# A chunked recurrence written out over one short and four long chunks, in place of a loop over six chunks of 88

## The chip, the cores and the metric

The kernel runs on one core of a Trainium2 chip. The metric is the device time of one execution in microseconds (us); each kernel is timed in several runs and the median is quoted. TensorE (PE in the rows) multiplies, VectorE (DVE) and ScalarE (ACT) work elementwise and copy results out of the accumulator memory (`ps`), GpSimd (POOL) and the DMA queues take no part in the stage that changes.

## What is computed

The reference is a two-block hybrid network on 512 tokens with 16 meta tokens in front (528 positions). The change is in one branch of the second block, a gated delta rule with 4 heads of width 128, run once forward and once backward over the positions. In the reference's words, for each chunk of positions:

```python
decay_mask = jnp.exp(jnp.where(lower, diff, -jnp.inf))
m = jnp.where(strict, jnp.einsum('bhnck,bhnsk->bhncs', k_beta, k) * decay_mask, 0.0)
t = lax.linalg.triangular_solve(eye + m, jnp.broadcast_to(eye, m.shape), left_side=True,
                                lower=True, unit_diagonal=True)
u = t @ v_beta
w = t @ (k_beta * jnp.exp(gc)[..., None])
...
def step(S, xs):
    v_new = u_n - w_n @ S
    o = qd_n @ S + attn_n @ v_new
    S = S * gl_n[..., None, None] + jnp.swapaxes(kd_n, -1, -2) @ v_new
```

The result does not depend on how long a chunk is: chunks of 88 or of 128 give the same sums, since the state S carries what came before.

## The kernel before

All float32. `phase_deltanet` is a stage by itself between the stage `Mixer` (projections, whose last matmul is at L239) and the stage `Rest` (its first instructions are ACT L2273 and PE L2247). It has four **flows**: two directions d times two pairs p of heads. Each flow has its own accumulator banks (two), its own tiles in `delta` and its own semaphore (`dn00` to `dn11`), which counts its finished steps.

The 528 positions are six chunks of CH = 88. PE, ACT and DVE each run a hardware loop (`Fori`) of six turns; one turn does one chunk of all four flows. The 46 names in `names` are the steps of a chunk in order, each on one engine. Each engine goes through its own steps in that order and does a step for flow 00, 01, 10, 11 before it goes on to its next step; before each it waits until that flow's semaphore says that the step before in `names` is done. The triangular inverse is built from products: `tr1` transposes, `p2`, `p4`, `p8`, `z4p` invert the diagonal blocks of 16, `fw`, `f2`, `f4`, `v1` to `v3` put them together, `ks` and `vn` form v_new, `o` the output and the state's update. Behind most of them ACT or DVE copies the result out (`tre`, `p2e`, ..., `vne`), since the next product reads it from SBUF. A product of two heads is two matmul instructions; each float32 matmul stands in the trace as two records of weight load (PEld) and of matmul (PE), a transposition as one.

At the start of a chunk DVE copies the decay row, k and v into `delta` (`stage`), PE spreads the row over the partitions (`bc`, L2409), and eight elementwise steps follow (`ebc` to `m4`, L2463, L2464, L2500 to L2508), with `gram` (L2412, L2413) among them, until `tr1` (L2416) can begin.

## Time and profile before

| | us |
|---|---|
| median of 3 runs | 3917.98 |
| lowest and highest | 3913.74, 3920.6 |
| the profiled execution | 3916.72 |
| its span in the trace | 3915.0 |

The span is the time between the first and the last instruction of the profiled execution; the 1.7 us beside it are launch and end. The page's first part gives the busy time of each engine. In the rows, "idle before" names what an engine waited for, and PEclk is the clock that TensorE was granted as a share of 2.4 GHz (0.50 would be 1.2 GHz throughout).

### The profile page before, as it was taken

To read this page: it belongs to the slowest core of one execution; us is meant where nothing else is said; L and a number is where in the kernel's file an instruction comes from. 1 tells how busy PE (TensorE), PEld (TensorE's weight loads), DVE (VectorE), ACT (ScalarE), POOL (GpSimd) and SP (SyncE) were. 2 spreads that over 40 slices of the span, in tenths; PEclk is the share of its full clock that TensorE was granted. 3 is DMA by queue.
4 is the path that set the end of the run, shared out by engine and by line. 5 is a ranking of instruction groups with operands and counts; after the bars stand their busy time and mean duration, and the time that the engine had idled before them with its cause. 6 is when DMAs were issued, how large, how long until landed. Compare 5 with 4: busy or idle time off the path is not lost. (4 is left out here: it accounts for less than half of the span.)

```text
span 3915.0 us, 55775 instructions
## 1 busy us (share of the span) xinstructions
PE 3669.0 (94%) x20346; PEld 3098.1 (79%) x20346; DVE 1871.6 (48%) x3703; ACT 1317.7 (34%) x2062; POOL 500.4 (13%) x429
## 2 busy tenths in 40 slices
PE   8988978999999999999999999979999888779997
PEld 8965467778888887888888899979887787658885
DVE  6333249936666423444444533345354455554333
ACT  3222322236666432222222332222223333333222
POOL 0000010443333200111111010110000000021011
PEclk9976789999999999999999999999999888889999
DMA  3200022435555644666666432322222000023331
GB/s 133 78 15 0 5 72 72 131 125 175 169 191 176 210 144 157 195 191 195 189 197 190 127 90 88 94 70 90 90 80 71 12 0 0 8 73 96 97 94 62
DMA packets 115321, 416.07 MB, mean 106 GB/s; under 512 B 14080, under 2 KB 14208, under 8 KB 112896
## 3 DMA queue, kind: packets, MB, share of 16 engines
q1 hardware_dynamic: 75520, 280.16, 23.3%
q0 software_dynamic: 18944, 67.12, 5.6%
q10 hardware_dynamic: 20736, 67.12, 4.5%
q8 instruction: 83, 1.36, 0.1%
q14 instruction: 38, 0.31, 0.0%
HBM read 345.14 MB, written 69.21 MB: 106 GB/s over the span
## 5 line engine op out<-in xcount | busy, mean ns | idle before, releaser
L755 DVE TENSOR_TENSOR w_lo<-ring,w_hi 128x1024 fp32r<-128x1024 f32 x224 | 275.3, 1229 | 697.2 <-ACT w_hi L751 697.2
L181 DVE TENSOR_TENSOR w_lo<-ring,w_hi 128x1024 fp32r<-128x1024 f32 (+2 forms) x173 | 225.1, 1302 | 605.8 <-ACT w_hi L175 605.8
L751 ACT ACTIVATE w_hi<-ring 128x1024 fp32r<-128x1024 f32 x256 | 271.1, 1059 | 516.9 <-PE ps L804 488.7
L774 PE MATMUL ps<-hn_hi,w_hi 128*128 128x512 f32 x1024 | 409.3, 400 | 17.2 <-POOL w_lo L755 16.2
L774 PE MATMUL ps<-hn_lo,w_hi 128*128 128x512 f32 x1024 | 405.5, 396 | 0.0
L774 PE MATMUL ps<-hn_hi,w_lo 128*128 128x512 f32 x1024 | 403.7, 394 | 0.0
L804 PE MATMUL ps<-units_hi,w_hi 128*128 128x512 f32 x1024 | 399.3, 390 | 2.7 <-DVE units_lo L1118 2.7
L804 PE MATMUL ps<-units_lo,w_hi 128*128 128x512 f32 x1024 | 398.9, 390 | 0.0
L804 PE MATMUL ps<-units_hi,w_lo 128*128 128x512 f32 x1024 | 398.9, 390 | 0.0
L175 ACT ACTIVATE w_hi<-ring 128x1024 fp32r<-128x1024 f32 (+2 forms) x173 | 193.1, 1117 | 420.0 <-PE ps L239 385.3
L239 PE MATMUL ps<-f_hn_hi,w_hi 128*128 128x264 f32 (+1 forms) x1056 | 284.6, 324 | 26.6 <-DVE f_hn_lo L1177 26.2
L239 PE MATMUL ps<-f_hn_lo,w_hi 128*128 128x264 f32 (+1 forms) x1056 | 284.8, 324 | 0.0
L239 PE MATMUL ps<-f_hn_hi,w_lo 128*128 128x264 f32 (+1 forms) x1056 | 283.7, 323 | 0.0
L774 PEld LDWEIGHTS ps<-hn_hi,w_hi 128*128 128x128 f32 x1024 | 193.3, 189 | 62.8 <-issue 16.1
L239 PE MATMUL ps<-hn_hi,mix_w_hi 128*128 128x264 f32 (+1 forms) x752 | 213.8, 335 | 23.5 <-DVE hn_lo L1177 19.5
L774 PEld LDWEIGHTS ps<-hn_hi,w_lo 128*128 128x128 f32 x1024 | 193.2, 189 | 43.8
L804 PEld LDWEIGHTS ps<-units_hi,w_hi 128*128 128x128 f32 x1024 | 192.6, 188 | 43.1 <-issue 3.1
L774 PEld LDWEIGHTS ps<-hn_lo,w_hi 128*128 128x128 f32 x1024 | 193.2, 189 | 42.2
L804 PEld LDWEIGHTS ps<-units_lo,w_hi 128*128 128x128 f32 x1024 | 192.6, 188 | 40.0
L804 PEld LDWEIGHTS ps<-units_hi,w_lo 128*128 128x128 f32 x1024 | 192.5, 188 | 40.1
L181 DVE TENSOR_TENSOR mix_w_lo<-ring,mix_w_hi 128x1024 fp32r<-128x1024 f32 (+2 forms) x73 | 97.4, 1335 | 245.0 <-ACT mix_w_hi L175 244.9
L239 PEld LDWEIGHTS ps<-f_hn_hi,w_hi 128*128 128x128 f32 x1056 | 177.3, 190 | 44.8 <-DVE w_lo L181 27.4
(409 smaller groups left out, 7139.1 us busy)
## 6 DMA issues: line engine op xcount, KB each, us to landing
ring<-in_w_uv SPq DMA_DIRECT2D x256, 512.0 KB, 3.7
ring<-in_f_up SPq DMA_DIRECT2D x88, 512.0 KB, 3.6
expert_units<-scratch ACTq DMA_DIRECT2D x128, 256.0 KB, 2.8
gate_table<-peer ACTq DMA_DIRECT2D x16, 2048.0 KB, 7.2
peer<-gate_table POOLq DMA_DIRECT2D x32, 1024.0 KB, 8.0
peer<-expert_units POOLq DMA_DIRECT2D x128, 256.0 KB, 3.6
ring<-in_w_in SPq DMA_DIRECT2D x29, 512.0 KB, 3.7
ring<-in_w_late SPq DMA_DIRECT2D x25, 512.0 KB, 3.6
```

Source lines behind the costliest of these rows:

```text
L175: self.nc.scalar.activation(self.h[:, self.slot(k), 0:self.cols], e.ring[:, self.ring(k), 0:self.cols], ACT.Copy).then_inc(e.hi_done, 1)
L181: self.nc.vector.tensor_tensor(self.l[:, self.slot(k), 0:self.cols], e.ring[:, self.ring(k), 0:self.cols], self.h[:, self.slot(k), 0:self. ...
L239: mm = nc.tensor.matmul(e.ps[:, bank + hf, 0:tokens.width], lhsT[:, wt.slot(k), col], rhs(part, c)[:, cut], start=(c == 0 and j == 0), sto ...
L751: A_(uh[:, slot(n)], e.ring[:, ring(n), 0:D], ACT.Copy).then_inc(e.hi_done, 1)
L755: ops.tensor_tensor(ul[:, slot(n)], e.ring[:, ring(n), 0:D], uh[:, slot(n)].bitcast(F32), ALU.subtract).then_inc(e.lo_done, 1)
L774: mm = M(e.ps[:, n % 2, :], u[:, slot(n), ch * P:(ch + 1) * P], x[part][:, ch, META:L], start=(ch == 0 and j == 0), stop=(ch == DC - 1 and ...
L804: mm = M(e.ps[:, o, :], v[:, slot(NK + g), col], w[:, g % 2], start=(first and j == 0), stop=(last and j == 2))
```

## The change

**Chunks.** In place of six chunks of 88 there is a first chunk of 16 (the meta columns) and four of 128. The forward flows do chunks 0 to 4; the backward flows do 4 to 1 and leave out chunk 0, whose backward output is not needed. In chunk 0 there is no state yet and no output, so that the forward flows have a shorter list there (`HEAD`, 21 groups).

**No loop.** The stage is written out; every position is a constant. `Chain` gives every step of a flow a turn: a full chunk has 28 groups (`GROUPS`), and each takes one turn, in chunk 0 half a turn. `turns` sorts all steps of the four flows by turn for each engine, and at the same turn by flow. The state's update before, k and v staged, and some other steps are merged or gone: `in` reads the decay row, k and q in place; `args`, `x1`, the state's update and `v1e` use an instruction that multiplies and adds at once (`scalar_tensor_tensor`, one head each); two copies of ACT become one over 512 columns (`tre`, `p2e`, `p4e`, `fwe`, `f2e`); the first direction to write a piece of the output copies instead of adding, and the clearing of the output is gone. A group of two names counts as done when both are.

**Elsewhere.** `Mixer`'s scans and decay columns run over the five chunks instead of six, and the column tables are cleared first.

```diff
-CH = 88
-NCH = L // CH
+CHUNKS = [(0, META)] + [(META + i * P, P) for i in range(T // P)]
+NCH = len(CHUNKS)
+FLOWS = [(0, 0, 0), (0, 1, 0), (1, 0, 0), (1, 1, 0)]
...
-            for n in range(NCH):
-                t = slice(n * CH, (n + 1) * CH)
-                ins = V.tensor_tensor_scan(g.cum[:, t], e.ones_row[0:16, 0:CH], g.t1[:, t], 0.0, ALU.mult, ALU.add)
+            for t0, m in CHUNKS:
+                t = slice(t0, t0 + m)
+                ins = V.tensor_tensor_scan(g.cum[:, t], e.ones_row[0:16, 0:m], g.t1[:, t], 0.0, ALU.mult, ALU.add)
...
-def phase_deltanet(nc, e, g, z, w, out):
...
+class Chain:
+    GROUPS = [("in",), ("args",), ("exps",), ("x1", "eb"), ("d",), ("fz",), ("tr1", "hold"), ("tre",), ("p2",),
+              ("p2e", "kd"), ("p4",), ("p4e", "z2"), ("p8",), ("p8e", "z3"), ("z4p",), ("z4",), ("fw",),
+              ("fwe", "zte"), ("f2",), ("f2e", "v1e"), ("f4",), ("f4e", "v2e"), ("v4",), ("v4e",), ("vn",), ("vne",),
+              ("o",), ("oe",)]
+    HEAD = [("in",), ("args",), ("exps",), ("x1",), ("fz",), ("tr1",), ("tre",), ("p2",), ("p2e", "kd"), ("p4",),
+            ("p4e", "z2"), ("p8",), ("p8e", "z3"), ("z4p",), ("z4",), ("fw",), ("zte",), ("vn",), ("vne",), ("o",),
+            ("oe",)]
+    ON = {"PE": ("in", "tr1", "p2", "p4", "p8", "z4p", "fw", "f2", "f4", "v4", "vn", "o"),
+          "ACT": ("exps", "eb", "tre", "p2e", "p4e", "p8e", "fwe", "f2e", "f4e", "vne")}
+    def __init__(self, sem, d, p, start):
+        self.sem, self.d, self.p = sem, d, p
+        self.before, self.turn = {}, {}
+        n = 0
+        if d:
+            self.before["zero", None], self.turn["zero", None], n = 0, start - 1, 1
+        at = start
+        for c in (range(len(CHUNKS)) if d == 0 else range(len(CHUNKS) - 1, 0, -1)):
+            for group in (self.GROUPS if c else self.HEAD):
+                for name in group:
+                    self.before[name, c], self.turn[name, c] = n, at
+                n += len(group)
+                at += 1 if c else 0.5
+    def wait(self, eng, name, c):
+        if self.before[name, c]:
+            eng.wait_ge(self.sem, self.before[name, c])
+def turns(flows, engine):
+    rest = Chain.ON["PE"] + Chain.ON["ACT"]
+    steps = [(f.turn[step], i, f, *step) for i, f in enumerate(flows) for step in f.before]
+    steps = [s for s in steps if (s[3] in Chain.ON[engine] if engine in Chain.ON else s[3] not in rest)]
+    return [s[2:] for s in sorted(steps, key=lambda s: s[:2])]
+def phase_delta(nc, e, g, z, w, out):
+    flows = [Chain(e.sem(f"dl{d}{p}"), d, p, start) for d, p, start in FLOWS]
...
+            for f, name, n in turns(flows, "PE"):
+                b = w[f.d, f.p]
+                t, m = chunk(n)
+                pair = slice(2 * f.p, 2 * f.p + 2)
+                k = kk[:, pair, t]
+                A, B, C, E = (place(f, j, m, m) for j in range(4))
+                wide = place(f, 3, m, P)
+                ident = c["ident"][0:m, 0:m]
+                U, V = ([cut(x[:, i], m) for i in range(2)] for x in (b.u, b.v))
+                zz, zt, D = cut(b.z, m), cut(b.et, m), cut(b.w, m) if n else V[1]
...
+                f.wait(pe, name, n)
+                if name == "in":
+                    row = (g.cum, g.back)[f.d][:, t]
+                    for h in range(2):
+                        i = 4 * f.d + 2 * f.p + h
+                        M(place(f, 0, P, m)[:, h], c["bc_g"][0:16, i * P:(i + 1) * P], row)
+                    mm = prod(C, k, k)
+                    if n:
+                        mm = prod(E, k, q[:, pair, t])
+                elif name == "tr1":
+                    for h in range(2):
+                        mm = TR(A[:, h], D[:, h], ident)
+                        if n:
+                            mm = TR(B[:, h], V[0][:, h], ident)
+                elif name == "p2":
+                    prod(A, U[0], D)
+                    prod(B, D, U[0])
+                    for h in range(2):
+                        mm = TR(wide[:, h], k[:, h], c["ident"])
+                elif name == "p4":
+                    prod(A, V[1], V[0])
+                    prod(B, V[0], V[1])
+                    mm = prod(C, V[1], zz)
+                elif name == "p8":
+                    prod(A, V[0], V[1])
+                    prod(C, V[1], zz)
+                    for h in range(2):
+                        mm = TR(wide[:, h], v[:, 2 * f.p + h, t], c["ident"])
+                elif name == "z4p":
+                    mm = prod(C, V[0], zz)
+                elif name == "fw":
+                    if n:
+                        prod(A, U[1], zz)
+                        prod(B, zz, U[1])
+                    for h in range(2):
+                        mm = TR(C[:, h], zz[:, h], ident)
+                elif name == "f2":
+                    prod(A, U[1], U[0])
+                    prod(B, U[0], U[1])
+                    prod(C, U[0], zt)
+                    mm = prod(wide, k, b.S)
+                elif name == "f4":
+                    prod(A, V[1], V[0])
+                    mm = prod(C, V[0], zt)
+                elif name == "v4":
+                    mm = prod(C, V[0], zt)
+                elif name == "vn":
+                    mm = prod(place(f, 0, m, P), zt, (b.z if n else b.w)[0:m])
+                elif name == "o":
+                    o, up = place(f, 2, P, m), place(f, 3, P, P)
+                    for h in range(2):
+                        if n:
+                            M(o[:, h], b.S[:, h], b.qd[:, h, 0:m], start=True, stop=False)
+                            M(o[:, h], b.w[0:m, h], b.at[0:m, h, 0:m], start=False, stop=True)
+                        mm = M(up[:, h], b.kd[0:m, h], b.w[0:m, h])
+                mm.then_inc(f.sem, 1)
...
+            for f, name, n in turns(flows, "ACT"):
+                b = w[f.d, f.p]
+                t, m = chunk(n)
+                A, AB = place(f, 0, m, m), both(f, m)
+                U, V = b.u[0:m, :, :, 0:m], b.v[0:m, :, :, 0:m]
+                f.wait(act, name, n)
+                if name == "exps":
+                    A_(cut(b.et, m), U[:, 0], ACT.Exp)
+                    ins = A_(V[:, 0], U[:, 1], ACT.Exp, scale=-1.0)
+                elif name == "eb":
+                    ins = A_(b.eb[:, :, 0:m], place(f, 0, P, m), ACT.Exp)
+                elif name in ("tre", "fwe"):
+                    ins = A_(U, AB, ACT.Copy) if n else A_(U[:, 0], A, ACT.Copy)
+                elif name in ("p2e", "p4e", "f2e"):
+                    ins = A_(V, AB, ACT.Copy)
+                elif name in ("p8e", "f4e"):
+                    ins = A_(V[:, 0], A, ACT.Copy)
+                elif name == "vne":
+                    ins = A_(b.w[0:m], place(f, 0, m, P), ACT.Copy)
+                ins.then_inc(f.sem, 1)
...
+                if name == "args":
+                    for i, x in enumerate((after, strict)):
+                        for h in range(2):
+                            ins = STT(out=U[:, i, h], in0=A[:, h], scalar=g.gcol[0:m, col + h:col + h + 1],
+                                      in1=x[f.d][0:m, 0:m], op0=ALU.subtract, op1=ALU.add)
+                elif name == "x1":
+                    for h in range(2):
+                        ins = STT(out=V[:, 1, h], in0=C[:, h], scalar=g.nbcol[0:m, col + h:col + h + 1],
+                                  in1=V[:, 0, h], op0=ALU.mult, op1=ALU.mult)
+                elif name == "d":
+                    ins = TT(b.w[0:m], V[:, 1], mask(c["sub"]), ALU.mult)
+                elif name == "fz":
+                    if n:
+                        TT(V[:, 0], V[:, 1], b.w[0:m], ALU.subtract)
+                    ins = TT(zz, b.w[0:m] if n else V[:, 1], mask(c["ident"]), ALU.add)
+                elif name == "hold":
+                    TT(b.at[0:m, :, 0:m], E, zt, ALU.mult)
+                    ins = TT(b.qd[:, :, 0:m], q[:, pair, t], b.eb[:, :, 0:m], ALU.mult)
+                elif name == "kd":
+                    ins = TT(b.kd[0:m], wide, over(b.et[0:m, :, edge]), ALU.mult)
+                elif name in ("z2", "z4"):
+                    ins = TT(zz, zz, C, ALU.add)
+                elif name == "z3":
+                    TT(zz, zz, C, ALU.add)
+                    ins = TT(b.w[0:m], wide, over(g.bcol[0:m, col:col + 2]), ALU.mult)
+                elif name == "zte":
+                    ins = V_.tensor_copy(zt, C)
+                elif name == "v1e":
+                    TT(zt, zt, C, ALU.add)
+                    for h in range(2):
+                        ins = STT(out=b.z[0:m, h], in0=wide[:, h], scalar=g.nbe[0:m, col + h:col + h + 1],
+                                  in1=b.w[0:m, h], op0=ALU.mult, op1=ALU.add)
+                elif name in ("v2e", "v4e"):
+                    ins = TT(zt, zt, C, ALU.add)
+                elif name == "oe" and n == 0:
+                    ins = V_.tensor_copy(b.S, place(f, 3, P, P))
+                elif name == "oe":
+                    if (f.p, n) in written:
+                        dve.wait_ge(*written[f.p, n])
+                        TT(out[:, pair, t], out[:, pair, t], place(f, 2, P, m), ALU.add)
+                    else:
+                        V_.tensor_copy(out[:, pair, t], place(f, 2, P, m))
+                        written[f.p, n] = (f.sem, f.before["oe", n] + 1)
+                    for h in range(2):
+                        ins = STT(out=b.S[:, h], in0=b.S[:, h], scalar=b.eb[:, h, edge:edge + 1],
+                                  in1=place(f, 3, P, P)[:, h], op0=ALU.mult, op1=ALU.add)
+                ins.then_inc(f.sem, 1)
...
+                x.u, x.v = a.take(2, 2, P), a.take(2, 2, P)
+                x.w, x.et, x.z, x.kd, x.qd, x.at, x.eb, x.S = (a.take(2, P) for _ in range(8))
```

Since all flows start at turn 0, but chunk 0 of the forward flows takes 10.5 turns, the forward flows are in another place of the chunk than the backward ones: 10.5 turns behind. The orders of PE and of ACT show it, at the start of the loop body before and in the middle of the stage after. First PE before (L2409 is `bc`, L2412 and L2413 are `gram`; `x8` is four flows by two heads):

```order
L2409 MATMUL ps<-delta,const_tab 128x88 x8
L117 REGISTER_ALU
L2412 MATMUL ps<-delta 88x88 x2
L2413 ISA
L2413 MATMUL ps<-z_12708,delta 88x88
```

All four flows do `bc` one after the other, and `gram` and `tr1` follow in the same way, with registers set between them. Now PE after, where the backward flow 11 (`dl11`) begins its second chunk; `dl00` and `dl01` are the forward flows:

```order
L2443 MATMUL ps<-gates,const_tab 128x128 [waits dl11]
L2443 MATMUL ps<-gates,const_tab 128x128
L2435 MATMUL ps<-z_12708 128x128 x4
L2435 MATMUL ps<-delta 128x128 [waits dl00]
L2435 MATMUL ps<-delta 128x128 x5
L2435 MATMUL ps<-delta,z_12708 128x128 x2
```

Behind the backward `in` stands the forward flows' `f2` (8 matmuls for each flow), then their `f4` and `v4`, and only then the backward `tr1`; before, nothing stood between. The other place is ACT, first before, behind `ebc` (L2463):

```order
L2463 ACTIVATE delta<-ps 128x176 [waits dn10]
L2463 ACTIVATE delta<-ps 128x176 [waits dn11]
L117 REGISTER_ALU
L2464 ACTIVATE delta<-delta 88x176 [waits dn00]
L2464 ACTIVATE delta<-delta 88x176
```

And ACT after, at the same point of the backward chunk:

```order
L2513 ACTIVATE delta<-ps 128x512 [waits dl00]
L2513 ACTIVATE delta<-ps 128x512 [waits dl01]
L2506 ACTIVATE delta<-delta 128x256 [waits dl10]
L2507 ACTIVATE delta<-delta 128x256
L2506 ACTIVATE delta<-delta 128x256 [waits dl11]
L2507 ACTIVATE delta<-delta 128x256
L2509 ACTIVATE delta<-ps 128x256 [waits dl10]
```

Before, the exponentials of all flows stood together; now the forward `f2e` (L2513) stands ahead of the backward `exps` (L2506, L2507) in ACT's queue.

## Rows read from the trace of the kernel before

**Rows 1.** The page: the span

```profile
span 3915.0 us, 55775 instructions
```

**Rows 2.** Windows of three loop turns and two parts: busy us (count), PEclk

```profile
core 0: us, PE busy (x) PEld busy (x) DVE busy (x) ACT busy (x) POOL busy (x), PEclk, DMA share, GB/s
3074.50:3128.00 53.50, 43.35 (x424) 42.29 (x424) 31.42 (x110) 18.82 (x65) 0.00 (x0) 0.85 0.00 1
3128.00:3181.80 53.80, 43.88 (x424) 42.85 (x424) 31.21 (x109) 18.81 (x65) 0.00 (x0) 0.85 0.00 0
3342.60:3398.00 55.40, 43.86 (x425) 42.83 (x426) 31.84 (x110) 18.25 (x66) 0.00 (x0) 0.84 0.00 0
...
3128.00:3146.00 18.00, 12.04 (x71) 11.50 (x72) 13.62 (x57) 4.40 (x16) 0.00 (x0) 0.59 0.00 0
3146.00:3170.00 24.00, 24.00 (x288) 23.92 (x287) 11.32 (x36) 11.61 (x44) 0.00 (x0) 0.96 0.00 0
```

**Rows 3.** Timeline at both ends of the stage: start, us, engine, line, instruction

```profile
3069.26 0.39 PE L239 MATMUL ps<-hn_hi,mix_w_lo 128*128 128x512 f32 x1
...
3071.81 1.82 DVE L2478 MEMSET scratch<- 128x2112 f32 x1 [1.43 <-PEq L1430]
...
3075.14 3.71 PE L2409 MATMUL ps<-delta,const_tab 16*128 16x88 f32 x16 [5.48 <-DVE delta L2499]
...
3395.58 1.41 DVE L2525 TENSOR_TENSOR delta<-delta,ps 128x256 f32<-128x256 f32 x4
3397.28 2.19 ACT L2273 ACTIVATE o_squares<-scratch 128x512 f32<-128x512 f32 x4 [8.37 <-PEq L2386]
```

**Rows 4.** Timeline of the second loop turn, its first third

```profile
3128.50 3.71 PE L2409 MATMUL ps<-delta,const_tab 16*128 16x88 f32 x16 [3.61 <-DVE delta L2499]
...
3134.48 0.89 PE L2412 MATMUL ps<-delta 128*88 128x88 f32 x4 [2.26 <-ACT delta L2464]
...
3141.94 0.52 PE L2416 MATMUL ps<-const_tab,delta 88*88 88x88 f32 x2 [3.19 <-DVE delta L2508]
```

**Rows 5.** The same turn, the part with PE unbroken

```profile
3147.72 11.03 PE L2423 MATMUL ps<-delta 88*88 88x88 f32 x136
...
3161.07 9.43 PE L2423 MATMUL ps<-delta 88*88 88x88 f32 x112
```

**Rows 6.** The same turn, its end: `r2`, `vn`, `vne`, `o`

```profile
3170.99 1.42 DVE L2518 TENSOR_TENSOR delta<-delta 88x256 f32<-88x256 f32 x4
...
3171.45 1.98 PE L2423 MATMUL ps<-delta 88*88 88x128 f32 x16 [0.95 <-DVE delta L2518]
3172.16 1.69 ACT L2472 ACTIVATE delta<-ps 88x256 f32<-88x256 f32 x4 [6.82 <-PE ps L2423]
3173.16 0.30 PEld L2445 LDWEIGHTS ps<-delta 128*128 128x128 f32 x2
...
3173.39 0.30 PEld L2446 LDWEIGHTS ps<-delta 88*128 88x128 f32 x2
...
3173.61 0.30 PEld L2447 LDWEIGHTS ps<-delta 88*128 88x128 f32 x2
...
3173.83 0.30 PEld L2445 LDWEIGHTS ps<-delta 128*128 128x128 f32 x2
```

**Rows 7.** Groups of instructions by line, one shape each: busy us, mean ns

```profile
L2516 DVE TENSOR_TENSOR delta<-delta,ps 88x176 f32<-88x176 f32 x72 | 22.7, 333 | 19.1 <-PE ps L2423 19.1
...
L2466 ACT ACTIVATE delta<-ps 88x176 f32<-88x176 f32 x48 | 12.4, 308 | 3.1 <-PE ps L2423 0.8
...
L2517 DVE TENSOR_TENSOR delta<-ps,gates 88x256 f32<-88x256 f32 x24 | 10.1, 421 | 1.6 <-PE ps L2423 1.3
...
L2472 ACT ACTIVATE delta<-ps 88x256 f32<-88x256 f32 x24 | 9.1, 379 | 42.0 <-PE ps L2423 40.9
```

**Rows 8.** The same view of the whole span: nearest shapes elsewhere

```profile
L850 ACT ACTIVATE scratch<-ps 128x512 f32<-128x512 f32 x128 | 76.5, 598 | 378.3 <-PE ps L774 378.2
...
L1055 DVE SCALAR_TENSOR_TENSOR peer<-peer 128x128 f32<-128x128 f32 x4 | 1.2, 293 | 0.1
L455 DVE SCALAR_TENSOR_TENSOR scratch<-ps,scratch 128x144 f32<-128x144 f32 x4 | 1.2, 307 | 8.8 <-PE ps L379 8.8
...
L1754 DVE TENSOR_TENSOR_SCAN gates<-misc,scratch 16x88 f32<-16x88 f32 x6 | 1.5, 308 | 0.0
```

**Rows 9.** DMA queues in the first loop turn, 3074 to 3128 us

```profile
DMA packets 4, 0.06 MB, mean 1 GB/s; under 512 B 0, under 2 KB 0, under 8 KB 0
...
q8 instruction: 3, 0.05, 0.4%
q14 instruction: 1, 0.01, 0.0%
```

210 lines of the change are left out of this document (51 added, 159 removed).

## The prediction

> **What bounds the kernel now.** I read the page first, for the span [rows 1], then windows of one loop turn each over the stage that changes, then the timeline at its ends and through one turn, then the groups by line for single durations. The stage stands alone: the last matmul of Mixer starts at 3069.26, the first work of the stage is DVE's memset at 3071.81, the last is DVE's L2525, which ends at 3395.58 + 1.41 = 3397.0, and Rest begins right after it [rows 3]. So the stage lasts 3397.0 - 3071.8 = 325.2 us, and all of it counts: no other work runs beside it. Each of the six turns takes some 54 us, with PE busy 43 to 44, DVE 31, ACT 19, at a mean granted clock of 0.84 to 0.85 [rows 2]. No engine is full. PE is idle before `bc` (3.61 us, for DVE's staging), before `gram` (2.26) and before `tr1` (3.19, for DVE's eight elementwise steps) [rows 4]; from `p2` on it runs nearly unbroken [rows 5], and it waits shortly again at the end of the turn. The granted clock falls with those idle stretches: the first third of a turn holds the gaps and also the slow matmuls. The reader is to see in rows 2 and 4 that a turn is PE's work plus the gaps plus the low clock that follows the gaps.
>
> **The change, part by part.**
>
> *PE's work.* The number of instructions per chunk and flow stays: 48 products (`in` 6, `p2` 4, `p4` 6, `p8` 4, `z4p` 2, `fw` 4, `f2` 8, `f4` 4, `v4` 2, `vn` 2, `o` 6) and 10 transpositions. Before there are 24 chunk-flows, now 16 long ones and 2 short. A product of 88 rows and columns takes two records of 11.03/136 = 0.081 us, so 0.16 us [rows 5]. What a wide one takes is seen in `o`, where weights are 128 wide: its weight loads start at 3173.16, 3173.39, 3173.61 and 3173.83, so 0.225 us for each product, whether 88 or 128 columns are streamed [rows 6]. `vn`, 128 columns by 88-wide weights, gives (1.98 - 0.28)/15 = 0.113 a record, the same. I take 0.225 for a product and half of it, 0.11, for a transposition: 48 x 0.225 + 10 x 0.11 = 11.9 us a chunk-flow at full clock, 47.7 for the four flows, 190 for the 16. Before it was 24 x (40 x 0.16 + 8 x 0.225 + 10 x 0.08) = 216. So PE's own work falls by only 26 us; the rest has to come from the gaps and the clock.
>
> *ACT.* 88 x 176 takes 308 ns, 88 x 256 takes 379 [rows 7], 128 x 512 from the accumulators takes 598 [rows 8]. A flow's chunk has five copies of 512 columns and six instructions of 256: 5 x 0.6 + 6 x 0.36 = 5.2, 21 us for four flows, no bound.
>
> *DVE.* 88 x 176 takes 333 ns and 88 x 256 takes 421 [rows 7]; in a queue the second follows after (1.42 - 0.41)/3 = 0.34 [rows 6]. The fused instruction over 128 columns takes 293 to 307 ns [rows 8]; less the same overlap of 0.08, 0.22. A flow's chunk (14 instructions of 256 columns, 10 fused ones, a copy) is 7.3 us, 29 for four flows, no bound either.
>
> *Latencies.* From a flow's last record of `vn` to ACT: 3171.45 + 4 x 0.112 = 3171.90, ACT starts at 3172.16, so 0.27. From DVE to PE: the first `r2` ends at 3170.99 + 0.41, PE starts at 3171.45, so 0.05 [rows 6].
>
> *The period.* The four flows repeat every 28 turns, forward 10.5 turns behind backward. I went through one period, each engine strictly in its queue's order, with these durations, at full clock, from the backward `in` at 0. PE: backward `in` to 2.7; forward `f2` to 6.3; ACT cannot start the backward `exps` before the forward `f2e` of the second flow, 7.2, so backward `x1` comes at 8 to 9.1 and forward `v2e`, behind it on DVE, ends at 9.8; forward `f4` ends at 8.35 and `v4` waits till 9.7 (idle 1.35); backward `fz` ends at 11.2, `tr1` to 12.4 (idle 0.9); forward `vn`; `hold` and `tre`, backward `p2` from 13.95 (idle 0.65) to 16.2; forward `o` to 18.9; backward `p4` to 21.6; forward `in` to 24.3; backward `p8` to 26.55; `z4p` waits 0.5 for `p8e`, and `fw` from 28.0 to 29.5 for `z4`, which stands behind forward `x1` and `d` on DVE; `tr1`, backward `f2`, and from there on no wait but 0.3, since the forward `p2` to `fw` fall between the backward `f4` to `o`. The period ends at 53.2: 47.7 of work and 5.5 idle.
>
> *The ends.* Up to the first forward `in` of a long chunk the short chunk runs with only the backward flows beside it: a period's first 21.6 us less the forward work (9.9), but bound by single waits. By the same walk 20 us at full clock and 27 at half; I take 24. From there: 53.2 - 21.6 = 31.6, three periods 159.6, and a tail with only forward flows from `f2` to the last `oe`, 11.8. Together 227. The largest gap in the period is 1.5 us where before it was 3.2 to 3.6; I add 3 us for clock lost anyhow: 230. PE can start at once at 3071.8, since `in` reads `gates` and `z` and no longer waits for DVE until 3075.14 [rows 3]; this is in the comparison already. The gain is 325.2 - 230 = 95 us.
>
> *Edits at nothing.* Mixer's six scans of 308 ns [rows 8] become five, with two short memsets behind them, and its decay columns go from six chunks to five: a few tenths each way beside the projections' matmuls of that stage; uncovered they would cost below 1 us. The registers of the loop go with the gaps already counted.
>
> *Straight-line code.* In its first turn the loop's code had to be fetched too: 4 packets of 0.06 MB in all [rows 9], and that turn took 53.5 us against 53.8 for the second [rows 2]. So I put nothing. The Trainium skill ("Runtime: NRT & Kernel Launch", section "Instruction fetch mechanics") says that the sequencer streams straight code by itself, mostly hidden, and that taken branches are what breaks the prefetch; the first turn agrees, and by that rule the sum is the same.
>
> *Clock.* Before, the low clock in each turn sits with the gaps [rows 2, 4]: `gram`'s first four records take 0.89 us for 88 columns where the unbroken part has 0.081 each [rows 4, 5]. The Trainium skill ("TensorE: Matmul & The Clock Gate", Part 1) says that half rate is the default and that activity releases it. If short gaps were enough to bring it back, it would speak against my 3 us; that case is a rival, priced from the rows.
>
> Sum against the profiled execution: 3916.7 - 95 = 3822 us. Its time is 1.3 below the median of 3917.98, which does not matter here.
>
> **The rivals.**
>
> 1. *Forecast*: period 53, clock near full. 3822, own range 3808 to 3838. Chance 0.61.
> 2. *The clock keeps falling.* Many gaps of 0.3 to 1.5 us remain in the first 14 us of a period. If the mean clock stays at 0.84 as before [rows 2], 190 us of work become 226: 33 more than forecast, 3855. For it: the first 18 us of a turn, with 0.59. Against: during 24 us of unbroken work before, PE was granted 0.96 [rows 2], and the gaps are half as long. Chance 0.17.
> 3. *Two flows do not cover the latencies.* If each of the 14 hand-overs of a chunk cost 0.6 us more on PE than I walked through, a period is 61 and the stage 34 longer: 3856. Against: DVE and ACT are at 29 and 21 of 53. Chance 0.08.
> 4. *Less waiting.* If PE never waits in the period and the beginning is at full clock, 22 + 4 + 3 less: 3793 to 3800. Chance 0.1.
> 5. *The change does not do what it says*: the flows are not in lock-step but 10.5 turns apart, and if one direction holds the other up in the in-order queues all the time, a period is a chain of two pairs, some 25 us of steps each plus waits, near 60: as rival 3 and with its chance.
> 6. *Slower than before.* Short passes with gaps never bring the clock up, and the whole stage runs at 1.2 GHz: 2 x 190 of work and some 37 of waits are 417, 92 more than before, 4009. It decides from a mean granted clock of 190/(325 - 37) = 0.66 on; below it the change loses. For it: the first 18 us of a turn have 0.59 [rows 2]. Against: mean 0.84 with longer gaps. Chance 0.02. Fetching the longer code, a stall at each packet, would need 16 KB packets at several us each to get there; 0.02 for a cost of 20 to 40 us, inside rival 2's times.
>
> **How the numbers follow.** A measurement of this kernel tells some 0.2%, 8 us, from no change. All cases but the last lie far below. Range: from the end of case 4, 3799, to the price of cases 2 and 3 with a little, 3860; about 0.15 is left outside. Faster 0.97, within 0.2% 0.01, slower 0.02.
>
> **What would show it.** Right: the stage is 225 to 235 us; in a window of one period in the middle PE is busy over 45 of some 53 us, granted clock above 0.95; DVE near 30. The PE gaps stand before forward `v4` and backward `fw`, ended by DVE or ACT. Records of 128 x 128 products at 0.112 us. Wrong: a PEclk of 0.85 there (rival 2); a period above 57 with idle before many steps (rival 3); records of 0.13 us or more, by which 190 would grow in proportion; or the first part longer than 27 us.

## The result and the profile after

The changed kernel takes 3823.24 us (median of 4 runs, 3820.98 to 3826.63), the kernel before 3916.32 (4 runs) beside it: a ratio of 0.9762, 95% interval 0.9745 to 0.9779. The forecast was 3822 with a range of 3799 to 3860. The page gives the span of the profiled execution, 93.6 us less than in [rows 1], and the engines' busy time:

```profile
span 3821.4 us, 53300 instructions
...
PE 3623.6 (95%) x19604; PEld 3043.6 (80%) x19604; DVE 1821.4 (48%) x3482; ACT 1287.7 (34%) x1863; POOL 500.2 (13%) x429
```

The timeline of after at both ends of the stage, which answers to [rows 3] (start, us, engine, line, instruction):

```profile
3068.64 0.39 PE L240 MATMUL ps<-hn_hi,mix_w_lo 128*128 128x512 f32 x1
...
3070.71 0.58 PE L2443 MATMUL ps<-gates,const_tab 16*128 16x16 f32 x4 [1.69 <-PEq L1431]
...
3303.95 0.60 DVE L2591 SCALAR_TENSOR_TENSOR delta<-delta,ps 128x128 f32<-128x128 f32 x2
3304.84 2.19 ACT L2277 ACTIVATE o_squares<-scratch 128x512 f32<-128x512 f32 x4 [3.53 <-PEq L2417]
```

The stage runs from 3070.71 to 3303.95 + 0.60 = 3304.55: 233.8 us against 325.2 before, 91.4 less. The other 2.2 us of the span lie outside it; the stages ahead end some us earlier or later from one execution to the next (Mixer's last matmul starts between 3065.96 and 3072.72 in the traces of this document). The windows of after, cut where the first record of a long forward `in` (3096.15) and the backward `in` (3129.77 and so on) start, answer to [rows 2]; the columns are us, busy us and count of PE, PEld, DVE, ACT and POOL, PEclk, DMA share, GB/s:

```profile
3070.70:3096.15 25.45, 22.88 (x189) 18.59 (x189) 13.86 (x55) 8.94 (x26) 0.00 (x0) 0.66 0.00 1
3096.15:3129.77 33.62, 32.16 (x262) 31.02 (x261) 19.88 (x58) 11.90 (x26) 0.00 (x0) 0.95 0.01 1
3129.77:3184.05 54.28, 51.06 (x426) 48.22 (x425) 33.38 (x100) 19.54 (x44) 0.00 (x0) 1.00 0.01 2
...
3292.51:3304.60 12.09, 10.79 (x90) 10.03 (x88) 5.82 (x17) 3.32 (x7) 0.00 (x0) 1.00 0.01 1
```

The period is 54.3 us, and its other two windows read the same to 0.1 us. PE is busy for 51 of it at the full clock; DVE is busy for 33 and ACT for 20. In a turn before ([rows 2]), PE was idle for 10 us and its clock was 0.85; now it is idle for 3.2 and the clock is 1.00. All waits of PE over 0.4 us in the second whole period, from its timeline, answer to [rows 4]:

```profile
3194.01 1.16 PE L2435 MATMUL ps<-delta 128*128 128x128 f32 x8 [0.68 <-DVE delta L2580]
...
3195.69 0.33 PE L2449 MATMUL ps<-const_tab,delta 128*128 128x128 f32 x1 [0.52 <-DVE delta L2561]
...
3198.32 1.16 PE L2435 MATMUL ps<-delta 128*128 128x128 f32 x8 [0.41 <-ACT delta L2511]
...
3214.72 1.16 PE L2435 MATMUL ps<-delta 128*128 128x128 f32 x8 [1.32 <-DVE delta L2568]
```

In order these are forward `v4` (for `v2e`, L2580), backward `tr1` (for `fz`, L2561), backward `p2` (for `tre`, L2511) and backward `fw` (for `z4`, L2568): four of the places that the walk through the period named. A row's time runs to the modelled end of its last record, 0.2 to 0.3 us past the point at which a next record could have begun, so that a wait in brackets is at least that much shorter than the time in which PE has nothing to issue.

### The profile page after: what moved, and what is told of

Its sections match the earlier page's. It is cut to its first block and busy times, and to the rows that moved or that the text cites. A ratio compares the mean times of both kernels' runs of the same rounds, so it can differ in the third digit from the quotient of the medians.

```text
span 3821.4 us, 53300 instructions
## 1 busy us (share of the span) xinstructions
PE 3623.6 (95%) x19604; PEld 3043.6 (80%) x19604; DVE 1821.4 (48%) x3482; ACT 1287.7 (34%) x1863; POOL 500.2 (13%) x429
## 5 line engine op out<-in xcount | busy, mean ns | idle before, releaser
L775 PE MATMUL ps<-hn_hi,w_hi 128*128 128x512 f32 x1024 | 409.2, 400 | 17.3 <-POOL w_lo L756 15.6
```

Of the source, the lines that this page charges most:

```text
L775: mm = M(e.ps[:, n % 2, :], u[:, slot(n), ch * P:(ch + 1) * P], x[part][:, ch, META:L], start=(ch == 0 and j == 0), stop=(ch == DC - 1 and ...
```

## The experiments

Each starts from the changed kernel unless it says otherwise. "Apart" is the distance of the two directions in turns of a 28-turn chunk; the change has 10.5. "Stage" in this section is the time in one trace from the start of Mixer's last matmul to Rest's first instruction, 3304.84 - 3068.64 = 236.2 us in after and 3397.28 - 3069.26 = 328.0 before; it leaves out how the other stages differ from one execution to the next. Kernels before and with the experiment ran on the same chip; the kernel before took 3915.4 to 3917.4 us each time.

### The four flows in the same place

```diff
-FLOWS = [(0, 0, 0), (0, 1, 0), (1, 0, 0), (1, 1, 0)]
+FLOWS = [(0, 0, 0), (0, 1, 0), (1, 0, 10.5), (1, 1, 10.5)]
```

> All four flows in the same place of the chunk: the backward flows begin 10.5 turns later, when the forward ones begin their first long chunk. My theory (what counts is that one pair's products fall into the other pair's elementwise stretch): the walk gives 47.7 us of products, 1.5 for the changes between 16-row and 128-row weights, and some 7 us in which PE waits from the end of in to p2, so a period of 56 to 57 at full clock, 59 to 60 with the clock falling in that gap, against 54.3 measured for the changed kernel; the first part is some 12 us instead of 25, so the stage takes about 250 us instead of 234 and the kernel 3835 to 3842. Rival (the distance between the flows is of no use, four flows in step cover each other as well): period 54, stage 228, kernel about 3817.

3832.44 us (3831.66 to 3833.41), ratio 0.9782 (0.9766 to 0.9799): 9 us above the changed kernel, a little less than expected and far from the rival; the stage is 3316.68 - 3069.00 = 247.7 us, 11.5 longer. The windows of this kernel, the second long chunk cut up, and the gap in its timeline:

```profile
3145.61:3151.00 5.39, 5.39 (x39) 4.67 (x39) 3.30 (x12) 1.40 (x4) 0.00 (x0) 1.00 0.00 0
3151.00:3156.00 5.00, 1.57 (x12) 1.26 (x11) 4.40 (x17) 2.58 (x9) 0.00 (x0) 1.00 0.00 0
3156.00:3161.00 5.00, 3.13 (x15) 3.13 (x16) 5.00 (x16) 0.47 (x1) 0.00 (x0) 0.56 0.00 0
3161.00:3166.00 5.00, 5.00 (x36) 4.97 (x35) 2.46 (x8) 3.23 (x7) 0.00 (x0) 0.76 0.01 3
3166.00:3202.57 36.57, 36.57 (x329) 36.45 (x327) 18.45 (x51) 12.83 (x26) 0.00 (x0) 1.00 0.01 1
```

```profile
3157.87 0.48 PE L2449 MATMUL ps<-const_tab,delta 128*128 128x128 f32 x1 [5.29 <-DVE delta L2561]
```

With all four flows in one place nothing stands between `in` and `tr1`, and PE waits for DVE's elementwise steps once a chunk, for 5.3 us. The clock falls behind the gap (0.56, then 0.76) and is back at 1.00 from 3166 on. The long chunks take 61.6, 57.0, 55.9 and 58.0 us.

### The directions 14 turns apart

```diff
-FLOWS = [(0, 0, 0), (0, 1, 0), (1, 0, 0), (1, 1, 0)]
+FLOWS = [(0, 0, 3.5), (0, 1, 3.5), (1, 0, 0), (1, 1, 0)]
```

> The two directions half a chunk apart, 14 turns instead of 10.5. My theory: any large distance fills the gaps; the period stays between 53 and 55.5, and the 3.5 turns with only one pair at both ends add 3 to 5 us: 3822 to 3832. Rival (the waits depend on what exactly stands ahead in the queues of ACT and DVE at each place): a period of 57 or more, 3840 and up, or 52 or less, 3815 and below.

3820.80 us (3816.54 to 3822.68), ratio 0.9750 (0.9733 to 0.9766). One period, from the windows of this kernel:

```profile
3106.83:3158.67 51.84, 49.85 (x424) 47.98 (x425) 32.79 (x99) 19.48 (x43) 0.00 (x0) 1.00 0.01 1
```

The period is 2.4 us shorter than in the change. It is below the 53 to 55.5 that I expected and in the rival's range (52 or less), while the kernel's time lies between the two, and its interval overlaps that of the change. The trace is plainer: the stage is 3303.74 - 3072.72 = 231.0 us, 5.2 less than in after. Three periods save 7.3, and the ends take 2.1 back. So the rival was right that the waits depend on what stands ahead in the queues, and my walk, made for one arrangement, did not look for the better one.

### The same order with chunks of 88

Six chunks of 88 for every flow, written out, with the merged steps and the flows 10.5 turns apart. What differs from the change is the length of the chunks, and with it that there is no short first chunk and that the backward flows do all six. Its main lines:

```diff
-CHUNKS = [(0, META)] + [(META + i * P, P) for i in range(T // P)]
+CHUNKS = [(i * 88, 88) for i in range(L // 88)]
...
-FLOWS = [(0, 0, 0), (0, 1, 0), (1, 0, 0), (1, 1, 0)]
+FLOWS = [(0, 0, 10.5), (0, 1, 10.5), (1, 0, 0), (1, 1, 0)]
...
```

> The changed kernel with its written-out order, merged steps and 10.5 turns of distance, but six chunks of 88 as before (both directions over all six, the forward flows later). Takes the chunk length alone back. My theory: PE has 36 + 1.5 us of work in a period and waits 6 to 7 as with 128, so 44 to 45 us a period, a stage of 270 to 280 and a kernel of 3858 to 3868: less than half of the 93 us come from the longer chunks. Rival A (only PE's own work counts): 26 us more, 3849. Rival B (the number of dependent steps sets the time, so the chunk length is nearly all of it): above 3890.

3919.49 us (3916.57 to 3923.59, 10 runs), ratio 1.0007 (0.9997 to 1.0016): no faster than the kernel before, and my expectation missed by 51 us. The time lies in rival B's range (above 3890), but not for B's reason, the number of dependent steps, as the windows show. Two of its periods, and then the first part of the one that begins at 3174.99 cut finer, all from its windows:

```profile
3174.99:3229.89 54.90, 52.16 (x425) 50.11 (x424) 27.83 (x100) 15.75 (x44) 0.00 (x0) 0.75 0.01 1
...
3286.84:3332.57 45.73, 43.12 (x425) 40.93 (x424) 27.75 (x100) 15.55 (x44) 0.00 (x0) 0.93 0.01 2
...
3181.00:3184.90 3.90, 2.68 (x26) 2.02 (x25) 3.78 (x16) 1.86 (x9) 0.00 (x0) 1.00 0.00 0
3184.90:3204.00 19.10, 19.10 (x109) 18.43 (x108) 5.86 (x22) 3.89 (x10) 0.00 (x0) 0.51 0.00 1
```

PE is idle for only 2.7 and 2.6 us in the two periods, and both hold the same 425 records. What differs is the clock. It falls behind three gaps of 0.3 to 0.5 us within 3.9 us, and then stays at the lower level (1.2 GHz) through 19.1 us in which the trace shows no idle time of PE. The timeline shows it in single instructions of one shape, eight records before and behind the fall, and between them the three gaps:

```profile
3180.43 0.79 PE L2435 MATMUL ps<-delta 88*88 88x88 f32 x8
...
3181.54 0.86 PE L2435 MATMUL ps<-delta 88*88 88x88 f32 x8 [0.32 <-DVE delta L2577]
...
3182.91 0.86 PE L2435 MATMUL ps<-delta 88*88 88x88 f32 x8 [0.51 <-DVE delta L2580]
...
3184.16 0.28 PE L2449 MATMUL ps<-const_tab,delta 88*88 88x88 f32 x1 [0.40 <-DVE delta L2561]
...
3188.07 1.38 PE L2435 MATMUL ps<-delta 88*88 88x88 f32 x8
```

The period from 3286.84 has the same three gaps (0.32, 0.51 and 0.40 us, the last before 3296.02), and there the clock stays at 1.00 up to 3305. The mean clock over the whole kernel is 0.935 or 0.936 in all ten runs, so that this is no accident of the profiled one. So here the low clock took the whole gain of the new order. Either short products bring it on, or this arrangement of the flows does; three of the later runs are about that.

### The kernel before, only written out

```diff
-            with pe.Fori(0, NCH) as it:
+            for it in range(NCH):
```

The same for ACT and DVE, with the positions as constants.

> The kernel before with its loop over six chunks written out, nothing else changed. My theory: registers, the branch back and fetching of code cost next to nothing either way, so 3908 to 3918 with turns of 53 to 54 us. Rival (the loop itself was a good part of the loss): below 3900. Other rival (straight code must be fetched and stalls): above 3925.

3909.45 us (3905.40 to 3915.22, 10 runs), ratio 0.9983 (0.9973 to 0.9992). A turn takes 53.06 us (window below) with the clock at 0.85 as before. By the interval, the registers and branches of the loop are worth 3 to 11 us, of 93; in the traces the stage is 3395.46 - 3071.00 = 324.5 us, 3.6 less than before.

```profile
3076.87:3129.93 53.06, 43.35 (x424) 42.35 (x424) 31.30 (x110) 17.54 (x64) 0.00 (x0) 0.85 0.00 1
```

### Two products more in `o`

```diff
+                        M(up[:, h], b.kd[0:m, h], b.w[0:m, h])
                         mm = M(up[:, h], b.kd[0:m, h], b.w[0:m, h])
```

> The changed kernel with the state's product in o issued twice (the second writes the same values): 2 more products for each of 18 chunk-flows, 0.45 us each. My theory (PE's own work is nearly the whole period): the period grows by 1.8 us and the kernel by 6 to 8 us, 3829 to 3831. Rival (chains of waits set the time and PE has slack): the period grows by less than 0.6, the kernel by less than 2.5.

3833.19 us (3831.40 to 3833.67), ratio 0.9789 (0.9775 to 0.9802).

```profile
3135.52:3191.58 56.06, 52.85 (x441) 50.00 (x440) 33.38 (x100) 19.55 (x44) 0.00 (x0) 1.00 0.01 1
```

Eight products more a period make it 1.78 us longer: 0.223 us for each, all of it on the path, as expected. So in the periods PE's own work sets the pace. The kernel, 10 us longer, missed the expected 6 to 8: its trace has a first part, up to the first long forward `in`, of 3102.40 - 3072.87 = 29.5 us at a granted clock of 0.60, where after has 25.45 at 0.66.

### ACT's copies of 512 columns in two halves

```diff
...
-                    ins = A_(V, AB, ACT.Copy)
+                    ins = (A_(V[:, 0], A, ACT.Copy), A_(V[:, 1], place(f, 1, m, m), ACT.Copy))[1]
```

The same for `tre` and `fwe`.

> The changed kernel with ACT's copies of 512 columns made as two of 256 again (tre, p2e, p4e, fwe, f2e). Each pair takes some 0.1 us longer than the one. My theory: ACT is off the path nearly everywhere, at most two of ten places in a period show the longer copy, so the period grows by 0 to 0.4 and the kernel by 0 to 2 us. Rival (ACT's latency is exposed at each hand-over): the period grows by 1 us or more, the kernel by 4 or more.

3826.21 us (3822.08 to 3826.88), ratio 0.9769 (0.9756 to 0.9782); the period is 54.39, 0.12 longer, with 20 copies more in it. The kernel's median is 3.0 us above that of the change, 1 more than expected, with intervals that overlap. By the period, that two copies became one is worth next to nothing in time; ACT is off the path nearly everywhere.

```profile
3133.95:3188.34 54.39, 51.05 (x425) 48.21 (x425) 33.38 (x100) 20.80 (x64) 0.00 (x0) 1.00 0.01 2
```

### The 16-row products of both flows side by side

`in` of the first flow of a pair also issues the spreading products of the second one, after waiting for it.

```diff
-                    for h in range(2):
-                        i = 4 * f.d + 2 * f.p + h
-                        M(place(f, 0, P, m)[:, h], c["bc_g"][0:16, i * P:(i + 1) * P], row)
+                    if f.p == 0:
+                        mate = next(x for x in flows if x.d == f.d and x.p == 1)
+                        mate.wait(pe, name, n)
+                        for x in (f, mate):
+                            for h in range(2):
+                                i = 4 * x.d + 2 * x.p + h
+                                M(place(x, 0, P, m)[:, h], c["bc_g"][0:16, i * P:(i + 1) * P], row)
```

> The changed kernel with the 16-row products of a pair of flows issued together, ahead of both flows' other products in in. My theory, from the trace after: each change between 16-row and 128-row weights costs PE some 0.2 us, eight in a period now and four then, so the period falls by 0.6 to 0.8 us and the kernel by 2.5 to 3.5. Rival (the slower records of in come from reading gates and z in place): the period stays at 54.2 to 54.3.

3817.64 us (3814.06 to 3825.85), ratio 0.9748 (0.9734 to 0.9761). The median is 5.6 us below that of the change, but the intervals overlap, so that the periods have to show it. One takes 53.51 us, 0.77 less than in the change, as expected; the next takes 54.89:

```profile
3155.21:3208.72 53.51, 50.27 (x426) 47.93 (x425) 33.12 (x100) 19.47 (x44) 0.00 (x0) 1.00 0.00 1
3208.72:3263.61 54.89, 51.65 (x426) 49.52 (x425) 33.20 (x100) 19.47 (x44) 0.00 (x0) 0.97 0.00 1
```

The same products are issued, and read the same tiles. What is saved is four of the eight changes between weights of 16 and of 128 rows, 0.19 us each: eight records with 16-row weights in a row take 3209.80 - 3208.72 = 1.08 us, 0.18 over 0.90, so that the extra time comes once with the change and not with each such product. The longer period has the clock in it. Behind a wait that stands in the other periods too, the clock is 0.56 to 0.59 from 3216.72 to 3220.72, and then 1.00 again:

```profile
3216.96 2.07 PE L2435 MATMUL ps<-delta 128*128 128x128 f32 x8 [1.32 <-DVE delta L2572]
```

So with chunks of 128, too, the clock can fall at this offset, for some 4 us.

### Chunks of 88 with useless products added

To the kernel with chunks of 88, 10.5 turns apart, two products ahead of `p2`, `p4` and `fw` of every flow, which are overwritten before anything reads them.

```diff
+                if name in ("p2", "p4", "fw"):
+                    for h in range(2):
+                        M(place(f, 1, P, m)[:, h], c["ident"], c["ident"][:, 0:m])
```

> Chunks of 88 as in the run whose periods stayed near 54.9 us at a granted clock of 0.75, with two extra products (identity weights, 88 columns, overwritten afterwards) ahead of p2, p4 and fw of every flow: 24 more products a period, at most 5.4 us at the full clock by 0.225 us each. Theory A: the low clock, and not waiting, is what takes the worth of the 88 columns away, and it hangs on how little TensorE has to do; then more work raises the clock to 0.9 or more, the period falls from 54.9 to about 51 us, and the kernel becomes faster than the run without the extra products, 3880 to 3905 us against 3919.5. Theory B: the clock stays at about 0.75 whatever is added; then a period is 54.9 + 5.4 / 0.6 to 0.75, 61 to 64 us, and the kernel takes 3955 to 3975 us. In between (3920 to 3950) the clock rises by less than the added work costs.

3916.29 us (3900.16 to 3919.18, 10 runs), ratio 0.9994 (0.9983 to 1.0004): outside both forecasts, and outside the range between them (3920 to 3950); two of the ten runs, at a mean clock of 0.950 against 0.946 or 0.947 in the others, took 3900 and 3905, the others 3914 to 3919. The windows show why the total says so little:

```profile
3117.56:3180.89 63.33, 60.59 (x473) 58.49 (x472) 27.92 (x100) 15.72 (x44) 0.00 (x0) 0.73 0.00 1
3180.89:3228.59 47.70, 45.09 (x474) 42.90 (x473) 27.83 (x100) 15.31 (x44) 0.00 (x0) 1.00 0.01 2
3228.59:3276.28 47.69, 45.08 (x473) 42.90 (x472) 27.84 (x100) 15.31 (x44) 0.00 (x0) 1.00 0.01 2
```

The period at 0.73 has the 63 us of theory B; three periods at 1.00 take 47.7, 7 us less than without the 48 records more, and shorter than theory A's 51. One program with the same order has both. The gaps that stood ahead of the fall in the run without the added products stand here too, in each period. In the period from 3117.56 the clock falls behind them (they come before 3124.11, 3125.48 and 3126.73, and the clock is 0.50 from 3131 on); in this one, from 3228.59, it stays up:

```profile
3235.15 0.86 PE L2435 MATMUL ps<-delta 88*88 88x88 f32 x8 [0.32 <-DVE delta L2580]
...
3236.51 0.86 PE L2435 MATMUL ps<-delta 88*88 88x88 f32 x8 [0.50 <-DVE delta L2583]
...
3237.76 0.28 PE L2452 MATMUL ps<-const_tab,delta 88*88 88x88 f32 x1 [0.40 <-DVE delta L2564]
```

PE is idle for 2.7 us in the one period and for 2.6 in the other, so that the clock, and no wait, makes the 15.6 us between them; what makes it fall is not shown.

### The directions 7 turns apart

```diff
-FLOWS = [(0, 0, 0), (0, 1, 0), (1, 0, 0), (1, 1, 0)]
+FLOWS = [(0, 0, 0), (0, 1, 0), (1, 0, 3.5), (1, 1, 3.5)]
```

> Chunks of 128, but the backward pair starts 3.5 steps late instead of the forward pair being a half turn behind, so that the two directions stand 7 places of the 14 apart, mirrored. Theory: the period hangs on TensorE's own work as long as the directions are some places apart; then the long periods are 52 to 55 us, the clock stays at 1.00, and the kernel is within 10 us of the changed one (3815 to 3833 us). Rival: only the offset of the change hides the waits of the steps; then gaps of 1 to 3 us appear at v4, tr1 and fw, the period is 57 us or more with a clock under 1.00, and the kernel takes 3838 us or more.

3815.30 us (3814.83 to 3820.14), ratio 0.9743 (0.9729 to 0.9758). One period from its windows, and its last row in the stage's timeline, Rest's first instruction (the stage begins at 3068.03):

```profile
3136.57:3188.36 51.79, 50.06 (x425) 48.05 (x424) 33.33 (x100) 19.99 (x44) 0.00 (x0) 1.00 0.00 1
```

```profile
3298.41 2.19 ACT L2277 ACTIVATE o_squares<-scratch 128x512 f32<-128x512 f32 x4 [3.53 <-PEq L2417]
```

PE is idle for 1.7 us a period. The period is 0.2 under the expected 52 to 55; the time is in the theory's range. The stage is 3298.41 - 3065.96 = 232.5 us, 3.7 less than in after.

### Chunks of 88, 7 turns apart

To the kernel with chunks of 88, one line:

```diff
-FLOWS = [(0, 0, 10.5), (0, 1, 10.5), (1, 0, 0), (1, 1, 0)]
+FLOWS = [(0, 0, 7), (0, 1, 7), (1, 0, 0), (1, 1, 0)]
```

> Six chunks of 88 written out as before, but the forward pair 7 turns behind the backward pair instead of 10.5, which made the shortest period with chunks of 128. It asks whether the low clock with 88 columns belongs to the short products or to one arrangement of the flows. Theory A, it belongs to the short products: periods again 53 to 57 us at a granted clock of 0.65 to 0.8, and the kernel 3900 to 3925 us (3.5 turns less of 1.96 us are 7 us below 3919.5). Theory B, it belongs to the arrangement: the periods are 43 to 46 us at 0.95 or more, as one period of that run was (45.73 at 0.93), the stage about 275 to 290 us, and the kernel 3865 to 3885 us. Then longer chunks would be worth 50 to 60 us less than the comparison so far says.

3843.91 us (3842.57 to 3844.19), ratio 0.9816 (0.9801 to 0.9831): 76 us less than 10.5 turns apart, and 21 less than even theory B's range. Two windows, and all waits of PE over 0.2 us in the period from 3197.39, from its timeline:

```profile
3115.34:3156.37 41.03, 39.26 (x426) 37.55 (x425) 27.70 (x100) 16.06 (x44) 0.00 (x0) 1.00 0.01 1
...
3197.39:3238.42 41.03, 39.26 (x426) 37.54 (x425) 27.69 (x100) 16.05 (x44) 0.00 (x0) 1.00 0.01 2
```

```profile
3201.53 1.11 PE L2435 MATMUL ps<-delta 88*88 88x128 f32 x8 [0.67 <-DVE delta L2580]
...
3211.03 2.74 PE L2435 MATMUL ps<-delta 88*88 88x88 f32 x32 [0.33 <-ACT delta L2513]
...
3216.16 1.75 PE L2435 MATMUL ps<-delta 88*88 88x88 f32 x16 [0.71 <-DVE delta L2571]
...
3326.72 2.19 ACT L2277 ACTIVATE o_squares<-scratch 128x512 f32<-128x512 f32 x4 [3.70 <-PEq L2417]
```

The same instructions of the same length; only FLOWS differs. The clock is 1.00 from 3115 on, and the period 41.03; the mean clock of the whole kernel is 0.954 or 0.955 in all four runs. Short products by themselves do not hold the clock down.

### The two short periods with the rows together

Both edits of the rows-together run and of the one 14 turns apart:

> The two edits that made the kernel shortest, together: the forward pair 3.5 steps late (period 51.84 us in its own run, kernel 3820.8) and the 16-row products of both flows of a pair side by side (0.77 us less a period in its own run). Theory: the second is TensorE's own time, so that it comes off here too: period 51.0 to 51.2 us, kernel 3814 to 3819 us, against 3823.2 for the changed kernel. Rival: with the waits of this offset between the flows the waiting for both flows' rows costs what the saved weight changes give; then the period stays at 51.8 us and the kernel at 3820 to 3823 us.

3814.89 us (3813.09 to 3817.63, 5 runs), ratio 0.9742 (0.9728 to 0.9755). And the rows together with 7 turns:

> Chunks of 128, backward pair 3.5 steps late (period 51.79 us in its own run, kernel 3815.3) and the 16-row products of both flows of a pair side by side, which took 0.77 us off a period of the changed kernel but only 0.2 off one with the forward pair late. Theory: part of the saved weight changes comes back as waiting for the later flow's rows, as there: period 51.0 to 51.6 us, kernel 3811 to 3816 us. Rival: the backward pair late leaves no slack for it and the period grows to 52 us or more, kernel 3816 to 3822 us.

3814.30 us (3811.52 to 3816.18, 5 runs), ratio 0.9742 (0.9729 to 0.9756). A period of each, first 14 and then 7 turns apart:

```profile
3150.57:3202.19 51.62, 49.12 (x426) 47.69 (x425) 32.89 (x100) 19.87 (x44) 0.00 (x0) 1.00 0.01 1
```

```profile
3134.70:3186.28 51.58, 49.33 (x425) 47.76 (x424) 33.06 (x100) 20.00 (x44) 0.00 (x0) 1.00 0.01 2
```

PE's busy time falls by 0.73 us in both (49.85 to 49.12, 50.06 to 49.33), but the period only by 0.2: 0.5 comes back as idle time. In the run 14 turns apart 0.23 of it is a new wait before the 16-row products, for DVE's update of a state (L2595), which the first flow did not have to wait for alone; the rest are longer waits before `fw` (0.79 for 0.65) and before `f2` (0.37 for 0.23). The first expectation's 51.0 to 51.2 missed that; the second took it in. By their stages these two are the shortest, 3294.96 - 3066.04 = 228.9 and 3295.94 - 3066.34 = 229.6 us, ahead of 231.0 (14 turns) and 232.5 (7 turns). By their medians these two and the one 7 turns apart are 8 to 9 us (0.2%) below the changed kernel, with intervals that overlap its own, and are not to be told from each other.

## Why the prediction was right, point by point

**The stage alone.** Right: 91.4 of the span's 93.6 us come from it. Forecast 230, measured 233.8; 2.2 us outside the stage, which the sum had at nothing (PE starts at 3070.71, 1.1 us earlier than the stage before, is half of it), brought the total to within 1.2 us. That the total is so close is luck: the stage was 3.8 us over its forecast, and half of those 1.1 us is only that Mixer's last matmul starts 0.6 us earlier in this trace.

**PE's own work, 26 us less.** Right in size, by a comparison that the forecast did not have: with 88 and with 128 columns, both 7 turns apart and with periods at the full clock, the time from the first product to Rest is 3326.72 - 3070.60 = 256.1 and 3298.41 - 3068.03 = 230.4, a difference of 25.7 us (28.6 between the medians of the kernels). That is not the term alone, and its closeness is partly luck: six periods of 41.03 against four of 51.79 differ by 39.0, and the short chunk, whose products the 26 left out, takes 13 back together with the ends. The 0.225 for a product was measured as 0.223.

**The rest from gaps and clock.** Right. A turn before is 53.50 us with PE busy for 43.35 [rows 2]; 88 columns, 7 turns apart, is 41.03 with 39.26. Of the 12.5 us a turn, 8.4 are idle time and 4.1 PE's busy time at a higher clock. The loop itself has little part in it (3 to 11 us for all six turns by its own run). How much of the 12.5 comes from the merged steps and how much from the order was not tested apart.

**The period, 53.2.** It was 54.3. The waits stood where they were forecast. In brackets they are 0.68, 0.52, 0.41 and 1.32 us for 1.35, 0.9, 0.65 and 1.5, but the walk counted from the point at which PE could issue again. By the starts of the rows and 0.112 a record they are longer. Ahead of the first and the last of the four stand (each with a short wait inside, since eight such records alone stand as 1.16 us)

```profile
3190.98 2.35 PE L2435 MATMUL ps<-delta 128*128 128x128 f32 x16
...
3211.86 1.54 PE L2435 MATMUL ps<-delta 128*128 128x128 f32 x8
```

so that PE has nothing to issue for 3194.01 - 3190.98 - 1.79 = 1.24 us before `v4`, and in the same way for 0.78 before `tr1`, 0.57 before `p2` and 3214.72 - 3211.86 - 0.90 = 1.96 from `z4p` to `fw`, where the walk had 0.5 and 1.5. All in all the waits are 54.3 - 47.7 - 1.5 (the changes of weights, below) = 5.1 for 5.5. The term that was mis-sized is `in`, taken as 6 products of 0.225, 1.35 us. These are two flows' `in` in the timeline of after:

```profile
3184.05 0.71 PE L2443 MATMUL ps<-gates,const_tab 16*128 16x128 f32 x4
...
3184.68 1.16 PE L2435 MATMUL ps<-z 128*128 128x128 f32 x8
...
3185.77 0.71 PE L2443 MATMUL ps<-gates,const_tab 16*128 16x128 f32 x4
```

From 3184.05 to 3185.77 it is 1.72 us: four records with 16-row weights take 0.63 and not 0.45, eight behind them 1.09 and not 0.90. That is 0.37 a flow and 1.5 a period, less 0.4 that the shorter waits gave back: 53.2 + 1.5 - 0.4 = 54.3. The rows-together run shows that it hangs on the changes, for it took four of the eight away and 0.77 us with them. A change between weights of 88 and of 128 rows shows no such cost (with chunks of 88, twelve records of 88 rows take 3178.61 - 3177.68 = 0.93 us up to the first of 128, no more than 12 of 0.081); why one of 16 does is not shown. The Trainium skill ("TensorE: Matmul & The Clock Gate", section "LDWEIGHTS (loading the stationary operand)") says that loading weights of few rows takes as long as of 128, since only the columns count. By that alone each record here would be 0.112, an estimate from that section's rule and the length of the other records; the trace has 0.18 to 0.19 more at each change, so the loading may be equal but the change is not free.

**The ends.** The first part took 25.45 us for 24, inside the 20 to 27 of its bounds (clock 0.66); the part up to the first whole period 33.6 for 31.6, at 0.95; the tail 12.0 for 11.8. The 3 us for clock were spent there and not in the periods, where it is 1.00 throughout in this trace. The first part is the favourable end of what can happen: in the runs with two products more, with split copies and with the rows together, all with the flows as in the change, it took 29.5, 28.5 and 29.6 us at clocks of 0.60, 0.58 and 0.54, over the 27 that the prediction named as a sign of being wrong.

**DVE, ACT, fetching, Mixer.** 33 and 20 us a period for 29 and 21; DVE's term was 4 us too small, without effect on the period. Split copies cost 0.12 us a period. Written out, the kernel before is no slower, so that the longer code shows no stall there.

**The rivals.** For this kernel rival 2 (the clock keeps falling) is out, since PEclk is 1.00. But its mechanism was real and close: the same order with chunks of 88 ran at 0.75 with PE idle for only 2.7 us a period, and lost 76 us by it against another offset, and with chunks of 128 and the rows together the clock fell once, for 1.4 us of time. I argued against it from 24 us of unbroken work at 0.96 [rows 2]; the run with 19.1 us at 0.51 shows that unbroken work alone is no such argument. That it did not come true here is in part luck, as nothing in the forecast tells why one offset has it and another not. Rival 3 would need a period of 61, rival 4 a period without waits, and rival 6 the lower clock throughout the stage. Rival 5's fear, that directions in different places hold each other up, is turned round: being apart is worth 9 us over being in one place at 10.5 turns, and 17 at 7.

**The split of the gain.** Of the 93 us: the long chunks are worth 26 to 29 where the clock is full, and 96 where it is not (3919.5 against 3823.2, 10.5 turns apart); writing out 3 to 11; the merged steps and the flows apart the rest, not told from each other. With 10.5 turns apart neither half of the change shows its own size, because the clock is in both. With 7 turns apart it does: order, merged steps and writing out give 72 us (3915.4 to 3843.9), the longer chunks 29 more.

**What stays open.** Why the clock falls with chunks of 88 at 10.5 turns and not at 7, and why with 128 at 10.5 turns only once in the traces of whole periods. Gaps are no sufficient reason: in one and the same kernel, waits of 0.3, 0.5 and 0.4 us within 3 us stand ahead of a fall in one period and in another at 1.00, and the wait of 1.32 us with chunks of 128 has a fall behind it in one period of the rows-together run and none in the others or in after. The Trainium skill (the same page, section "HAM oscillation — how this bites in real kernels") describes the clock falling in long waits and coming back with work. The run with the flows in one place fits that (5.29 us, then 0.56, then 1.00); the chunks of 88 do not: the longest wait in their whole periods was 1.07 us, and work did not bring it back for 19 us.

## What to carry to other kernels

Walk one period through the in-order queues, engine by engine, before writing a schedule: it named all the waits over 0.4 us here, and the offset between independent chains is then worth trying at several values, since it moved kernels of the same instructions by up to 17 us with chunks of 128 and by 76 with 88. Judge a rewrite by windows with their granted clock, and never by one arrangement alone; a kernel whose busy share is high can be one that runs at half the clock. Group the products whose weights have few rows, if nothing has to wait for it.

## What was not expected of the hardware

- PE without idle time for 19.1 us at a granted clock of 0.51, behind waits of at most 0.5 us; behind the same waits in another period of the same kernel 1.00.
- 48 useless matmul records a period, and three periods 7 us shorter than without them (47.7 at 1.00, 54.9 at 0.75), another 8 us longer (63.3 at 0.73), and no gain in the kernel.
- Each change between weights of 16 rows and of 128 costs PE 0.19 us, with float32 records of 0.112 us; one between 88 and 128 shows no cost.
